# Seven of eight TensorE turns of 128x512 block pairs replaced by a path through DRAM and VectorE

## What is computed

```python
def hybrid_mixer(h, w_in, ...):
    proj = h @ w_in
    z, xbc, dt_raw, q, k, v, g, gk_lr, gate_ssd, gate_gla = _split_cols(proj, IN_SPLIT_SIZES)
    ...
    y = ssd_chunked(xh, dt, A, Bm, Cm) + ssd_D[:, None] * xh      # 64 heads in 8 groups of 512 columns
    y = grouped_rms_norm(y * jax.nn.silu(z), ssd_norm_w, SSD_N_GROUPS)
    ...
    o = gla_chunked(q, k, v, gk)                                  # 4 heads of 512 columns
    o = grouped_rms_norm(o, gla_norm_w, 1) * jax.nn.silu(g)
    branch_ssd = y @ w_ssd_branch
    branch_gla = o @ w_gla_branch
    merged = (jax.nn.sigmoid(gate_ssd + gate_bias[0]) * branch_ssd
              + jax.nn.sigmoid(gate_gla + gate_bias[1]) * branch_gla)
    return merged @ w_out
```

## Time and profile before

| | |
|---|---|
| median of 3 runs | 2842.58 us (2839.41 to 2844.2) |
| profiled execution: time / span | 2843.83 / 2842.5 us |
| TensorE matmul busy (by the profile's modelled ends) | 2818.7 us, 99% |
| weight loads of TensorE | 2335.3 us, 82% |
| VectorE | 1841.9 us, 65% |
| ScalarE | 1445.1 us, 51% |
| GpSimd | 198.4 us, 7% |
| DMA | 667.71 MB, mean 235 GB/s; 65709 packets under 512 B |

### The profile page before, as it was taken

The page is one execution under the profiler, slowest core; times in us unless marked ns, Lnnn a source line. Parts: engine busy times, 40 slices in busy tenths (PEclk is TensorE's granted clock), DMA queues, the critical chain, the costliest instruction groups (busy, mean ns, idle before and its releaser), DMA issues. The chain is left out here.

```text
span 2842.5 us, 34753 instructions
## 1 busy us (share of the span) xinstructions
PE 2818.7 (99%) x13414; PEld 2335.3 (82%) x13414; DVE 1841.9 (65%) x2311; ACT 1445.1 (51%) x1959; POOL 198.4 (7%) x309
## 2 busy tenths in 40 slices
PE   9999999999999999999999999999999999999998
PEld 8888888888888878888888888888888888888887
DVE  6477787777755757567656556565666556676556
ACT  5455565556554655444444434344545445645544
POOL 1200000000000000000102001020000020000110
PEclk9999999999999999999999999999999999999999
DMA  7778888888877778775767676676576667776675
GB/s 254 244 254 277 267 290 284 278 281 282 257 230 236 249 230 293 240 254 165 255 212 222 207 207 208 207 229 200 170 266 204 216 213 225 221 230 220 219 219 184
DMA packets 386148, 667.71 MB, mean 235 GB/s; under 512 B 65709, under 2 KB 95261, under 8 KB 384958
## 3 DMA queue, kind: packets, MB, share of 16 engines
q1 hardware_dynamic: 271104, 510.33, 56.0%
q10 hardware_dynamic: 97614, 104.65, 11.7%
q0 software_dynamic: 17264, 50.50, 5.5%
HBM read 609.34 MB, written 56.03 MB: 234 GB/s over the span
## 5 line engine op out<-in xcount | busy, mean ns | idle before, releaser
L1673 DVE TENSOR_TENSOR w_lo<-raw,w_hi 128x1024 fp32r<-128x1024 f32 (+2 forms) x976 | 1156.5, 1205 | 710.1 <-ACT w_hi L1015 702.7
L983 PE MATMUL bank<-w_lo,x_hi 128*128 128x512 f32 (+2 forms) x3888 | 1524.6, 392 | 8.5 <-DVE w_lo L1673 4.7
L985 PE MATMUL bank<-w_hi,x_lo 128*128 128x512 f32 (+2 forms) x3888 | 1508.0, 388 | 0.0
L984 PE MATMUL bank<-w_hi,x_hi 128*128 128x512 f32 (+2 forms) x3888 | 1507.2, 388 | 0.0
L1015 ACT ACTIVATE w_hi<-raw 128x1024 fp32r<-128x1024 f32 (+2 forms) x976 | 995.3, 1044 | 861.7 <-PE bank L985 370.3
L983 PEld LDWEIGHTS bank<-w_lo,x_hi 128*128 128x128 f32 x3888 | 730.8, 188 | 163.0 <-issue 9.6
L985 PEld LDWEIGHTS bank<-w_hi,x_lo 128*128 128x128 f32 x3888 | 730.4, 188 | 150.4
L984 PEld LDWEIGHTS bank<-w_hi,x_hi 128*128 128x128 f32 x3888 | 731.0, 188 | 147.3 <-issue 2.9
L1025 ACT ACTIVATE x_hi<-bank 128x512 fp32r<-128x512 f32 (+1 forms) x96 | 53.5, 587 | 159.2 <-PE bank L665 144.9
L231 POOL DMA_DIRECT2D hidden<-arena x96 | 61.7, 650 | 895.1 <-DVE arena L2415 894.3
L2494 POOL DMA_DIRECT2D proj<-stage x48 | 34.4, 717 | 1193.1 <-DVE stage L2358 688.0
(11 more groups left out here) (225 smaller groups left out, 1318.3 us busy)
## 6 DMA issues: line engine op xcount, KB each, us to landing
raw<-in_w_in SPq DMA_DIRECT2D x492, 512.0 KB, 5.0
raw<-in_w_up SPq DMA_DIRECT2D x128, 512.0 KB, 4.2
raw<-in_w_down SPq DMA_DIRECT2D x128, 512.0 KB, 4.5
raw<-in_w_out SPq DMA_DIRECT2D x96, 512.0 KB, 4.8
arena<-proj ACTq DMA_DIRECT2D x74, 512.0 KB, 5.3
raw<-in_w_ssd_branch SPq DMA_DIRECT2D x64, 512.0 KB, 5.4
proj<-stage POOLq DMA_DIRECT2D x48, 512.0 KB, 5.6
raw<-in_w_gla_branch SPq DMA_DIRECT2D x32, 512.0 KB, 4.9
```

The source lines that it names most:

```text
L983: pe.matmul(o, x_hi[:, xk, tokens(t)], w_lo[:, r, k, 0:b.n], start=a, stop=False)
L984: pe.matmul(o, x_hi[:, xk, tokens(t)], w_hi[:, r, k, 0:b.n], start=False, stop=False)
L985: op = pe.matmul(o, x_lo[:, xk, tokens(t)], w_hi[:, r, k, 0:b.n], start=False, stop=z_)
L1673: TT(w_lo[:, p % SPLIT_RING, 0:b.per, 0:b.n], raw[:, p % RAW_RING, 0:b.per, 0:b.n], w_hi[:, p % SPLIT_RING, 0:b.per, 0:b.n].bitcast(F32), ...
```

## The change

The upper SSD groups take the path of the lower ones: `ssd_group` on TensorE loses its turn, ScalarE stores every group's `xt` to `heads_y` at step 25, and a new stage `upper`, begun at piece 264, fetches group n = 0 to 3 into `halves` and turns it through bank 7 at pieces 270 + 10 n and 271 + 10 n (VectorE's transpose one piece earlier). `turned_lower` follows behind it. VectorE's first tap of a group waits for the landing of the store of the group before, instead of for its turn on TensorE.

`merged` of blocks 0 to 2 is stored by GpSimd's queue, fetched by ScalarE's queue at the eighth piece of the following block and turned by VectorE 2 pieces later; `high` and `lower` follow at 3 pieces. Block 3 is still turned by TensorE, now into banks 4 and 5. Since `gla_branch` 3 has `ends`, the stage of block 2, which begins at its last piece (423), runs to its end there.

```diff
@@ schedule @@
+    sides.append((at + 2, "upper", ()))
@@
+        if j < NB - 1:
+            beside(b, "merged", j, at=2 * KT // QK - 1)
@@ tensor: ssd_group @@
-            if g < SSD_UPPER:
-                yield SSD_STEP["out"]
-                pe.wait_ge(*ssd.dve["out", g])
-                for t in range(NT):
-                    turn(5 + t, xt[:, t, :]).then_inc(*ssd.pe("out", g, t))
@@ tensor: result @@
-            if b.kind == "gla_branch":
+            if b.kind == "gla_branch" and b.info[0] == NB - 1:
                 j = b.info[0]
                 for t in range(NT):
-                    if j:
-                        pe.wait_ge(*merge.dve["lo", j - 1, t])
                     pe.wait_ge(*merge.dve["merged", j, t])
-                    turn(6 + t, merged[:, b.half, t, :]).then_inc(*merge.pe("turned", j, t))
+                    turn(4 + t, merged[:, b.half, t, :]).then_inc(*merge.pe("turned", j, t))
@@ scalar: ssd_group @@
+            act.wait_ge(*ssd.dve["out", g])
+            turned_store(act.dma_start, heads_y[g], xt, lambda: side_out("heads_y", g))
+
+        def turned_upper():
+            def fetch(n):
+                act.dma_start(halves[n % 2], turned_rows(heads_y[n])).then_inc(*half_in[n % 2]("upper", n))
+
+            act.wait_ge(*side_out["heads_y", SSD_G - 1])
+            act.wait_ge(*ssd.pe["off", SSD_G - 1])
+            fetch(0)
+            fetch(1)
+            for n in range(SSD_UPPER):
                 for t in range(NT):
-                    act.wait_ge(*ssd.pe["out", g, t])
-                    high(5 + t, KT + 4 * g, t).then_inc(*ssd.act("hi", g, t))
+                    yield UPPER_FIRST + UPPER_PACE * n + t
+                    act.wait_ge(*turned.dve["turned", "upper", n, t])
+                    high(7, KT + 4 * n, t).then_inc(*turned.act("hi", "upper", n, t))
+                if n + 2 < SSD_UPPER:
+                    fetch(n + 2)
@@ scalar @@
+        def merged_turned(j):
+            act.wait_ge(*merge_out[j % 2][j])
+            if j:
+                act.wait_ge(*merge.dve["turned", j - 1, NT - 1])
+            act.dma_start(merged_in, turned_rows(merged_by_feature[j])).then_inc(*merge_in(j))
+            yield 3
+            if j == 0:
+                act.wait_ge(*summed[start_of["gla_branch", 0].first - 1])
+            for t in range(NT):
+                act.wait_ge(*merge.dve["turned", j, t])
+                high(6 + t, KT + 4 * j, t).then_inc(*merge.act("hi", j, t))
@@ vector: ssd_group @@
-                if g > SSD_UPPER:
+                if g:
                     dve.wait_ge(*side_out["heads_y", g - 1])
-                elif g:
-                    dve.wait_ge(*ssd.pe["out", g - 1, NT - 1])
@@ vector @@
+        def turned_upper():
+            for n in range(SSD_UPPER):
                 for t in range(NT):
-                    dve.wait_ge(*ssd.act["hi", g, t])
-                    lower(5 + t, KT + 4 * g, t).then_inc(*ssd.dve("lo", g, t))
+                    yield UPPER_FIRST + UPPER_PACE * n + t - 1
+                    dve.wait_ge(*half_in[n % 2]["upper", n])
+                    if n or t:
+                        dve.wait_ge(*turned.dve.now)
+                    turn(by_tile(bank[7]), halves[n % 2][:, :, tokens(t)]).then_inc(
+                        *turned.dve("turned", "upper", n, t))
+                    yield UPPER_FIRST + UPPER_PACE * n + t
+                    dve.wait_ge(*turned.act["hi", "upper", n, t])
+                    lower(7, KT + 4 * n, t).then_inc(*turned.dve("lo", "upper", n, t))
@@ gpsimd @@
+        for j in range(NB - 1):
+            pool.wait_ge(*merge.dve["merged", j, NT - 1])
+            turned_store(pool.dma_start, merged_by_feature[j], merged[:, start_of["gla_branch", j].half, :, :],
+                         lambda: merge_out[j % 2](j))
```

57 lines of the change are left out of this document (31 added, 26 removed).

## The result

The changed kernel takes 2859.71 us in the median of 4 runs (2853.0 to 2861.96), against 2843.24 us for the kernel before on the same chip (4 runs, the three of the table ahead and one more): ratio 1.0057, 95% interval 1.0037 to 1.0076. It is 0.57% slower, by more than the 0.2% that a measurement can tell from no change, and beyond the upper end of the predicted range (2843.5). The profiled execution took 2853.0 us, with a span of 2851.7 us, 9.2 us more than the span of before; it was the quickest of the four, and where the other 6 us of the median lie no trace shows. Of the runs further down, e13_ssd_spstores and e14_ssd_spread had one execution each at a lower granted clock (3917.1 us at 0.676, 3110.87 us at 0.853), and their medians leave it out.

The account below looks back on a forecast made before the run. Prediction: TensorE bound, with one thin spot in each SSD group. SSD -1.2, GLA start +0.5 and `merged` -3.2 us made -3.9 us, 2838.7 us in the median; range 2835.0 to 2843.5 us.

Parts of the forecast that it names:

- The sum: Whole kernel: SSD groups -1.2, start of GLA +0.5 and `merged` -3.2 us, together -3.9 us.
- The turns and their waits: `merged` 0 to 2: three turns leaving TensorE save 2.7 us, and the waits for two of them 1.0 us.
- The start of GLA: New stage among the GLA work, near piece 274: costs 0 to 2 us, +0.5 us taken.
- the lead of 2.2 us: Piece 274: its `w_lo` is ready at 778.2 us, TensorE begins it at 780.43; expected to be about used up.
- The wait for `merged` 3: At TensorE's one remaining turn of `merged`: `merged` 3 ready at 33.1 us, TensorE there at 32.7; about 0.5 us waited.
- The chain from `merged` 2 to `merged` 3: Store, landing, fetch, transposes, casts, last `w_lo`, then gate sum to branch sum, added up to 26.1 us.
- the fetches of `merged` 0 and 1 have a whole block of time ... they are hidden: `merged` blocks 0 and 1: fetches from DRAM cost nothing, with ScalarE 16 us ahead there.
- The SSD groups: Groups 0 to 3 without TensorE turns: -1.2 us, bounds -4.6 (all distances quiet, 74.53 us) to +1.9 (all like the worst).
- The store takes the place of that wait: SSD groups 0 to 3: ScalarE's 5.51 us of store issue replaces its 6.34 us wait for TensorE's turn; no new cost.
- ScalarE's stores make the weights a whole piece late: Rival, SSD groups 0 to 3: casts come 2.72 us late at each group; +4.6 us in all, 2847.2 us, chance 0.05.
- What would show it: Signs listed: 56 transposes fewer, `w_lo` waits at step 12, DMA share 0.86 or more, waits of at most 2 us.
- Above 76.5 (then the queue is): Sign of a wrong forecast: SSD group distances above 76.5 us would mean the queue, here of the stores, causes the waiting.

Follow-up runs that it names:

- e13_ssd_spstores: SSD half of the change alone (`merged` as before), stores of all eight groups on SyncE's queue instead of ScalarE's: 2878.27 us, ratio 1.0118 to the kernel before.
- e14_ssd_spread: SSD half of the change alone, each group's eight stores on ScalarE's queue in pairs, one pair a piece (group 7 all at once): 2872.04 us, ratio 1.0094.
- e1: Changed kernel with only its SSD half; `merged` turned on TensorE as in the kernel before: 2843.88 us, ratio 1.0005 to the kernel before.
- e3: Changed kernel, but the stage of `merged` 2 is not run to its end at piece 423: 2847.81 us, ratio 1.0019 to the kernel before.
- e4: The changed kernel measured once more, unchanged: 2853.39 us, ratio 1.0039 to the kernel before.
- e10: SSD half of the change alone, stores of all eight groups on GpSimd's queue, new stage left in place: 2834.60 us, ratio 0.9967 to the kernel before.
- e7_merge_pool: Kernel before plus `merged` half; GpSimd's queue issues fetches, `merged` 0 and 1 turned three pieces later, nothing run to its end: 2844.93 us, ratio 1.0005.
- e6_merge_two: Kernel before with `merged` 0 and 1 by DRAM, 2 and 3 turned on TensorE: 2846.71 us, ratio 1.0013 to the kernel before.
- e9_before_pool: Kernel before with only the stores of SSD groups 4 to 7 moved to GpSimd's queue: 2841.53 us, ratio 0.9992 to the kernel before.
- e8_ssd_pool: SSD half of the change alone, all eight groups' stores on GpSimd's queue, new stage moved to piece 272: 2831.44 us, ratio 0.9955 to the kernel before.

## Why the prediction was wrong

**The sum** was -3.9 us; the profiled execution shows +12 from piece 18 on. The turns held, the start of GLA came inside its bounds, the wait for `merged` 3 failed by far, and the account of the SSD groups failed in its mechanism.

**The turns and their waits** of `merged`: -3.7 predicted, -3.6 measured. The cost of a turn (0.89 us) and the reading of the two waits hold.

**The start of GLA**: +0.5 taken from 0 to 2, +1.3 measured; the five kernels with the stage where the change has it (after, e1, e3, e4, e10) lose 1.0 to 1.5 us from piece 272 to 275. Inside its bounds; the lead of 2.2 us was used up.

**The wait for `merged` 3**: +0.5 predicted, +12.4 measured, of which 9.5 us are the wait and 2.9 the clock after it. The step that failed is the chain's start, "`merged` 2 itself is ready 1.1 + 1.2 + 4.7 = 7.0 us after TensorE ends `gla_branch` 2". The chain from `merged` 2 to `merged` 3 was put at 26.1 us and took 27.5. But TensorE begins piece 416 at 1193.8 us in the kernel after, and `merged` 2 is complete at 1209.2, 15.4 us later. Part of this stood in the trace of before. Its VectorE timeline, which the prediction doesn't use:

```profile
1202.15 1.28 DVE L2004 TENSOR_TENSOR arena<-arena 128x512 f32<-128x512 f32 x2
...
1205.52 1.29 DVE L2400 TENSOR_TENSOR arena<-arena 128x512 f32<-128x512 f32 x2
```

TensorE began piece 416 at 1195.5 us there, so `merged` 2 was ready 11.3 us after it: the gate sum stands at the fourth piece of the next block, and I had counted only the work, not the place in the order. With 11.3 the same sum would have given 11.3 + 26.1 - 32.7 = 4.7 us of wait, and the forecast 0.3 us of loss in place of 3.9 of gain. The other 4.1 us is the same round trip one block earlier: the gate sum of `merged` 2 (1204.49) stands behind the turn of `merged` 1 (1199.83), which waited for a fetch issued at 1192.93. I wrote that "the fetches of `merged` 0 and 1 have a whole block of time ... they are hidden", and followed only the chain of `merged` 2. They were not, since the round trip is longer than a block: 26.0 us of period against 21.8. e7_merge_pool, in which this turn stands behind the gate sum and GpSimd's queue issues the fetch, has these 4 us back (11.2), and e6_merge_two moves the wait to `merged` 2. The last 1.4 us are the chain's own, 27.5 for 26.1. The forecast also had no term for the clock, 2.9 us.

**The SSD groups**: -1.2 predicted with -4.6 to +1.9 as bounds, +2.4 measured with the later groups (+1.3 in the four groups costed, inside the bounds; +1.1 in the three that the prediction left at zero). As a size this is weak, since profiles of the same SSD code lie several us apart, and e1_ssd_only, whose interval takes in -0.7 us, doesn't refute the forecast of this half. The method was at fault too: it read single distances of one trace as if they would return, and the last of them, 76.15 us, was 77.77, 77.39 and 75.25 in the three other profiles with the same code. The mechanism is what the runs decide. The sentence that failed is on ScalarE: "The store takes the place of that wait" (6.34 us for TensorE's turn) and so "is no new cost". It does take its place, 5.14 us of issue, but the next group's loads are queued behind it and then the casts of weights, where in the old order these stood behind a short `high`. The rival "ScalarE's stores make the weights a whole piece late" had the mechanism; its price, 2.72 us at each of four groups, was too high for the groups and its condition was met in two of them (2.4 and 3.3 us above quiet). I dismissed it since groups 4 to 7 "do this already and the distances don't show it". They do show it: 74.91, 75.21 and 76.15 become 74.53 each in e9_before_pool, where nothing but the queue of these stores, and with it their packets, changed. A stretch that pays a cost all the time was read as proof that it costs nothing.

**What would show it**: the 56 transposes fewer, waits at step 12 (and 13, where the 1.01 us of the earlier trace rows stands by this count) and a wait of under 1 us near piece 274 came as listed, and the DMA share rose to 0.85 where 0.86 was named. "Above 76.5 (then the queue is)" is met by two distances, and "a long wait at the first `w_out` block, which would mean the chain from `merged` 2 is longer than added up" by the 9.5 us, though the chain was nearly as long as added up (27.5 us against 26.1) and began later.

**On the rules.** The Trainium skill's "VectorE: DVE Perf Modes", Rules for kernel authors, which spoke for TensorE's turn, did not decide: with the stores on another queue the SSD half by VectorE is 0.45% faster (e8_ssd_pool), and TensorE is never idle from 143 to 747 us in it. VectorE's added work was on the path only near piece 273, for 1.0 to 1.5 us. The Trainium skill, "DMA: Bandwidth & Descriptors", Issuing engines are not separate DMA queues, says that another issuing engine saves only the sequencer's time, "which is usually small relative to the DMA itself". The trace agrees that the sequencer's time is what ScalarE saves, 5.14 us for eight stores, but here it was what the time hung on: the sequencer saved is the one that casts the weights, and it was worth some 10 us of 2844.

## What to carry over

On an engine that also computes, the issue of a DMA is work of that engine; charge it like an instruction, and put stores in many small runs on the queue of an engine that nothing waits for at that moment: GpSimd here, and not SyncE, which feeds the weights (2878 us). When a turn is replaced by a round trip through DRAM, add up the whole loop from one block's result to the next one's, with the place in the program's order at which each step stands, and compare it with the block's time on TensorE; if it is longer, every block makes the next one later. Read such a starting point from the trace where it stands, rather than rebuild it from durations. And before a wait of one trace is taken as the price of something, see how much it differs in another execution of the same code.

## What the runs showed of the hardware

- A TensorE that waited 9.5 us ran the next 4 us at a granted clock of 0.50 (1.2 GHz); after only 4.1 us of waiting, in e7_merge_pool, the row of the eight transposes is as long (1.97 us), at a granted clock of 0.74 from 1228 to 1232 us. The clock cost 2.9 us in the first case and 1.6 in the second (0.9 in the transposes each time, and 2.0 and 0.7 from piece 428 to 429), a third of the wait itself or a little more. Shorter waits did it at times: one of 1.84 us in e1_ssd_only (0.57 from 706 to 710 us) and one of 2.01 in e4_after_again (0.58 from 702 to 706), while after one of 1.80 in the kernel after it stayed at 1.00.
- The same eight stores of 64 KB in runs of 32 floats hold ScalarE's queue for 5.14 us, GpSimd's for 5.17, and SyncE's for 15.27 in group 0. GpSimd's took the same for every group, to within 0.1 us; SyncE's took 5.70 us for group 7, after which no next group's loads come.
- The time to issue a pair of them on ScalarE's queue was 0.85 us, and 4.29 and 5.09 us behind the loads of the next group; all eight at once took 6.66 us for group 7, which has no next group. The long issues came only where a next group's loads are. Whether these must stand on the same queue is open: in e13_ssd_spstores the long issues are on SyncE's queue and the next group's loads on ScalarE's.
- The same stores make fewer small packets when GpSimd issues them: 49901 packets under 512 B in e8_ssd_pool, with all eight groups stored, against 82669 in e1_ssd_only, with the same stores from ScalarE. The loads of weights took 5.1 us to land in both (143:445).
